# The two adaLN parts of a hybrid diffusion step: matmul rows on four column groups of TensorE instead of one, modulation on VectorE

## The chip, the core and the metric

One core of one Trainium2 chip runs the whole program. The metric is the device time of one execution in microseconds (us). The engines are PE (TensorE: matmuls; PEld are its weight loads), DVE (VectorE), ACT (ScalarE), POOL (GpSimd) and SP (SyncE, which issues most DMAs). All of them run their own list of instructions in order and meet at semaphores.

## What is computed

One layer of a diffusion backbone on 1024 latent tokens and 128 context tokens, width 1024, all in float32. The conditioning vector is multiplied by a 1024 x 6144 matrix, `w_ada`. Of the six slices of the result two (shift `sh1`, scale `sc1`) modulate the input of the first projection, `w_in`; the others are used behind the output projection and the feed-forward part.

```python
def trunk_layer(x, cond, rows, cols, st0, p):
    ada = jax.nn.silu(cond) @ p['w_ada'] + p['b_ada']
    sh1, sc1, g1, sh2, sc2, g2 = jnp.split(ada, 6, axis=-1)
    h = modulate(layer_norm(x), sh1, sc1)        # x * (1 + scale) + shift
    proj = h @ p['w_in']
    ...  # pooling mixer, convolution + bidirectional mLSTM scans, w_out
    x = layer_norm(ALPHA * x + g1[:, None, :] * mix, p['ln1_g'], p['ln1_b'])
    h = modulate(layer_norm(x), sh2, sc2)
    ffn = conv_ffn(h, rows, cols, p['w_up'], p['w_dw'], p['b_dw'], p['w_down'])
    x = layer_norm(ALPHA * x + g2[:, None, :] * ffn, p['ln2_g'], p['ln2_b'])
```

There are two conditioning vectors: `c` for the latent tokens and `c_ctx` for the context tokens. So `silu(cond) @ w_ada` is a product of two rows with a large matrix.

## The kernel before

Order and buffers are written out by hand for each engine; what is said here of an order is the order of that engine's code.

**The start.** SP loads nine token tiles `xt` (128 tokens each), between them the first four of eight loads of `w_ada` (load i: half of the contraction, 512 columns; `ADA1_BLOCKS` says which columns), then two units of `w_in` (`raw`), the last four loads of `w_ada` and two more units. DVE takes the statistics of each tile, ACT normalises it (`x_norm`), PE transposes it (`x_transposes`, eight 128 x 128 matmuls with the identity), and ACT copies the result out of PSUM into `xT` (`xT_evac`).

**adaLN, first part.** Loads 0, 1, 3, 4, 6 and 7 are multiplied on PE (`ada1_rows`): for each of the four 128-row slices in a load one matmul with the two conditioning columns in `colv` as weights and 512 columns of `w_ada` as moving operand. The result, two rows of 512, lies in partitions 0 and 1 of PSUM bank 6. Loads 2 and 5 are instead multiplied and summed on DVE (`ada1_acc`, one accumulator for each conditioning vector), and PE adds the 128 partitions of the accumulators onto the two rows (`ada1_fold`, weights `pick`). ACT copies the two rows into `arow` (`arow_evac`), PE transposes them block by block into bank 7 (`ada1_cols`), and DVE adds the bias (`ada1_evac`), once for each half of the 1024 channels. Then ACT modulates `xT` with scale and shift of each channel (`modulate`) and rounds it (`h1hi`), and DVE makes the rest `h1lo = xT - h1hi`: all large products are made from three fp32r matmuls, hi x hi, hi x lo and lo x hi. `h1_first` does the first of eight channel rows in three token groups, `h1_parts(k)` a whole row.

**First tiles of the projection** (`first_tiles(half, k)`): half 0 makes tiles 0 and 1 with channel rows 0 to 3 as far as row k goes, 18 matmuls of 384 columns; half 1 adds rows 4 to 7 of the other weights. Between them stand `ada1_fold(1)`, the rows of loads 6 and 7 and the last column transposes. Then come the gate columns and the other units of the projection, n = 4 to 31, with three token groups g each.

**adaLN, second part.** DVE multiplies and sums the other 3072 columns of `w_ada` in six blocks j beside the projection (`ada_unit`, 48 of them; each adds one 128-row slice for both conditioning vectors). When a block is summed, PE adds its partitions (`ada2_cols` by way of `acc_cols`, 8 matmuls): the accumulator is the weight, `pick` (two columns) the moving operand, and the result comes out as columns in bank 6. `ADA_COLS` puts the six behind token group 1 of units n = 5, 11, 16, 20 and 28, and behind the first group of the unit after the last. DVE waits for j before it starts the block that reuses the accumulator (`ada_unit`, the wait for `pe_ada`). Another 1024 columns come much later through `acc_cols` too; the change does not touch them.

The functions that the change touches, and what calls them:

Of the kernel before, what the change touches and what calls it, by code (L numbers as in the profile page):

```python
# [10 lines left out]
P = 128  # L11
# [52 lines left out]
ROW_BLOCKS = (2, 0, 3, 1)  # L64
ACC_LOADS = (2, 5)
# [55 lines left out]
def layer(nc, x_prompt, x_sample, c, state_C, state_n, state_m, c_ctx, w_ada, b_ada, w_in, b_gates,  # L121
          w_qk_conv, hn_g, w_pool, pool_scale, w_out, ln1_g, ln1_b, w_up, w_dw, b_dw, w_down,
          ln2_g, ln2_b, inv_count, y_prompt, y_sample, new_C, new_n, new_m, scan_rows, gate_rows, pool_out, x1_rows, u_rows, t_rows):
    with ExitStack() as stack, nc.allow_non_contiguous_dma(reason="normaliser column of the state, stabiliser rows"):
# [77 lines left out]
        grow = place("grow", [1, 2, P])  # L202
        mrow = place("mrow", [1, P])
# [16 lines left out]
        arow = place("arow", [2, 2, AC], tmp_at + 4 * 4 * AC + 8 * AC)  # L220
# [4 lines left out]
        aacc0 = place("aacc0", [P, 2, AC], M0 + 4 * (KT - 1) * T)  # L225
# [238 lines left out]
        nmr_ready, acc1_ready = sem("nmr_ready"), sem("acc1_ready")  # L464
# [4 lines left out]
        (x1_copied, x2_copied), X_0 = d_exp, NT  # L469
        s_kept, kw_kept, KEPT_0 = (ln_ready, exps_ready), (rows_silu, wghi_ready), 1  # L470
# [683 lines left out]
        def _(pe):  # L1154
# [15 lines left out]
            def ada1_rows(i, start):  # L1170

                pe.wait_ge(ada1_in[i % ADA1_RING], 16 * (i // ADA1_RING + 1))
                if start and i:
                    pe.wait_ge(arow_ready, i // 2)
                for k in range(KH):
                    kk = (i % 2) * KH + k
                    last = mm(ps[0:2, 6, :], colv[:, V_C + kk:V_CC + kk + 1:V_CC - V_C], adaw1[:, i % ADA1_RING, k, :],
                              start=(start and k == 0), stop=(not start and k == KH - 1))
                last.then_inc(pe_ada, 1)

            def ada1_fold(a):

                pe.wait_ge(acc1_ready, a + 1)
                for w in both:
                    last = mm(ps[0:2, 6, :], pick[:, w, :], (aacc0, aacc)[a][:, w, :], start=False, stop=(w == 1))
                last.then_inc(pe_ada, 1)

            def ada1_cols(j):

                pe.wait_ge(arow_ready, j + 1)  # L1190
                if j == 2:
                    pe.wait_ge(ada_a, 1)
                for b in range(AB):
                    blk = ROW_BLOCKS[j] * AB + b
                    last = nc.tensor.transpose(ps[:, 7, 2 * blk:2 * blk + 2], arow[:, j % 2, b * P:(b + 1) * P],
                                               ident[0:2, 0:2])
                return last
# [23 lines left out]
            ada1_fold(0)  # L1221
            x_transposes(8)
            ada1_cols(1).then_inc(pe_adaT, 1)
            ada1_rows(4, True)

            def ada2_cols(j):

                pe.wait_ge(ada_used, 4 * (j + 1))
                acc_cols(6, 2 * (4 + j) * AB, [ada_sum(j)[:, w, :] for w in both]).then_inc(pe_ada, 1)
# [557 lines left out]
        def _(act):  # L1787
# [36 lines left out]
            def modulate(k, spans):  # L1824
                for w, tok_ in spans:
                    last = fn(xT[:, k, tok_], xT[:, k, tok_], ACT.Identity,
                              scale=ada1p[:, 0, k, w:w + 1], bias=adaT[:, A_SH1 + k, w:w + 1])
                last.then_inc(mod_ready, 1)

            def h1_first():  # L1830
                act.wait_ge(xT_out, NT)
                act.wait_ge(ada_a, 1)
                for g in range(NG):
                    modulate(0, [(0, grp(g))] if g < NG - 1 else [(0, slice(g * GN, LAT)), (1, slice(LAT, T))])
                    act.wait_ge(mod_ready, g + 1)
                    fn(h1hi[:, 0, grp(g)], xT[:, 0, grp(g)], ACT.Copy).then_inc(h1hi_ready, 1)

            def h1_parts(k):
                if k == KH:
                    act.wait_ge(ada_a, 2)  # L1840
                modulate(k, ((0, slice(0, LAT)), (1, slice(LAT, T))))
# [27 lines left out]
            arow_evac(3)  # L1869
            for k in range(KH, KT):  # L1870
                h1_parts(k)
# [51 lines left out]

            for n in range(4, 2 * NPROJ):
# [42 lines left out]
            silu(2 * H - 1)  # L1967

# [710 lines left out]
        def _(dve):  # L2679
# [8 lines left out]
            v.memset(neghalf[:, :, :], -0.5).then_inc(ones_ready, 1)  # L2688

# [29 lines left out]
            def ada1_evac(half):  # L2719
                dve.wait_ge(pe_adaT, half + 1)  # L2720
                ada_evac(7, A_SH1 + half * KH, A_SH1 + (half + 1) * KH)
# [831 lines left out]
```

## Time and profile before

| | |
|---|---|
| time, median of 3 runs | 1291.76 us (1289.9 to 1292.05) |
| the profiled execution's own time | 1290.97 us |
| its span, first to last instruction | 1289.2 us |
| PE busy | 1241.7 us (96% of the span), 7531 matmul records |
| DVE busy | 1011.9 us (78%) |
| ACT busy | 583.2 us (45%) |
| POOL busy | 652.7 us (51%) |
| DMA | 210.25 MB, 163 GB/s in the mean |

The rest of 1.8 us lies around the span. A float32 matmul is two records on PE, each with a weight load; an fp32r matmul and a transpose are one. Times in rows count from the start of the span. A record of PE contains its way through the array, so records overlap: what one costs in a stream is the distance from its start to the next one's.

### The profile page before, as it was taken

How to read it: one execution, taken by the hardware profiler on the slowest of the kernel's cores; microseconds unless marked ns; L12 is line 12 of the kernel's file. 1: busy time of each engine (PE TensorE's matmuls, PEld its weight loads, DVE VectorE, ACT ScalarE, POOL GpSimd, SP SyncE). 2: the span in 40 equal slices, each digit the busy share in tenths (PEclk: the TensorE clock that was granted, in tenths of full speed). 3: DMA queues.
4: the chain of work that ended last, by engine and by line, in shares of the span. 5: the costliest groups of instructions: out<-in, count | busy, mean ns of one | idle time of the engine just before them, and what ended most of it. 6: DMA issues, size and time to landing. Idle time of an engine off the chain costs nothing.

```text
span 1289.2 us, 21414 instructions
## 1 busy us (share of the span) xinstructions
PE 1241.7 (96%) x7531; PEld 1131.1 (88%) x7531; DVE 1011.9 (78%) x1556; ACT 583.2 (45%) x1013; POOL 652.7 (51%) x519
## 2 busy tenths in 40 slices
PE   6899999999988999998999999999999999999996
PEld 3488899999987778998999999999999988888885
DVE  6466688965688788799878787878866599889898
ACT  5644112536546444555454444445434456345430
POOL 1001999604343011369798888879787764200011
PEclk9999999999999999999999999999999999999999
DMA  9524232463336532213635353544534669946882
GB/s 359 167 77 144 61 111 87 144 191 83 94 105 233 175 115 78 70 33 120 190 122 187 130 180 122 179 161 142 165 135 150 219 231 382 329 131 208 300 315 100
DMA packets 161777, 210.25 MB, mean 163 GB/s; under 512 B 10567, under 2 KB 98723, under 8 KB 161443
## 3 DMA queue, kind: packets, MB, share of 16 engines
q1 hardware_dynamic: 161214, 204.47, 48.3%
q0 software_dynamic: 288, 4.72, 0.9%
q8 instruction: 44, 0.72, 0.2%
q14 instruction: 34, 0.28, 0.1%
q10 hardware_dynamic: 197, 0.06, 0.0%
HBM read 161.49 MB, written 47.72 MB: 162 GB/s over the span
## 4 chain that ended last, share of the span: by engine, by line
PE 52%; POOL 2%; DVE 1%; issue 1%; ACT 0%; POOLq 0%
PE ps L1693 11%; PE ps L1691 11%; PE ps L1692 11%; PE ps L1724 6%; PE ps L1726 6%; PE ps L1725 6%; POOL tlo L2387 0%; POOL ulo L2387 0%; POOL xlo L2387 0%; POOL dwlo L2387 0%; POOL xwlo L2387 0%; PE ps L1203 0%; POOL wsum L2592 0%; DVE z L3434 0%; DVE z L3433 0%
## 5 line engine op out<-in xcount | busy, mean ns | idle before, releaser
L3248 DVE SCALAR_TENSOR_TENSOR ps<-gs,taps,ps 128x945 f32<-128x945 f32 (+2 forms) x176 | 215.7, 1226 | 10.0 <-ACT ps L2165 4.6
L2534 POOL TENSOR_TENSOR rstd<-mv,neghalf 128x1 f32<-128x1 f32 x27 | 24.8, 918 | 258.2 <-DVE mv L3425 156.9
L1296 PE MATMUL ps<-h1hi,whi 128*128 128x384 f32 x336 | 118.5, 353 | 0.9 <-DVE wlo L2731 0.9
L1724 PE MATMUL ps<-dwhi,uhi 128*128 128x512 f32 x290 | 113.0, 390 | 1.3 <-POOL dwlo L2387 1.3
L1726 PE MATMUL ps<-dwhi,ulo 128*128 128x512 f32 x290 | 112.9, 389 | 0.0
L1725 PE MATMUL ps<-dwlo,uhi 128*128 128x512 f32 x290 | 112.9, 389 | 0.0
L1296 PE MATMUL ps<-h1hi,wlo 128*128 128x384 f32 x336 | 112.5, 335 | 0.0
L1296 PE MATMUL ps<-h1lo,whi 128*128 128x384 f32 x336 | 112.4, 335 | 0.0
L2387 POOL TENSOR_TENSOR wlo<-raw,whi 128x512 fp32r<-128x512 f32 x40 | 57.2, 1431 | 80.8 <-ACT whi L1796 48.0
L1691 PE MATMUL ps<-thi,xhi 128*128 128x288 f32 x320 | 94.3, 295 | 2.0 <-issue 1.1
L1693 PE MATMUL ps<-thi,wlo 128*128 128x288 f32 x320 | 94.4, 295 | 0.0
L1693 PE MATMUL ps<-thi,xlo 128*128 128x288 f32 x320 | 94.4, 295 | 0.0
L1692 PE MATMUL ps<-tlo,whi 128*128 128x288 f32 x320 | 94.2, 294 | 0.0
L1692 PE MATMUL ps<-tlo,xhi 128*128 128x288 f32 x320 | 94.2, 294 | 0.0
L1691 PE MATMUL ps<-thi,whi 128*128 128x288 f32 x320 | 94.1, 294 | 0.0
L1691 PE MATMUL ps<-h2hi,whi 128*128 128x288 f32 x240 | 71.5, 298 | 1.0 <-POOL wlo L2387 1.0
L1691 PE MATMUL ps<-h2hi,xhi 128*128 128x288 f32 x240 | 70.8, 295 | 1.2 <-POOL xlo L2387 1.2
L1693 PE MATMUL ps<-h2hi,wlo 128*128 128x288 f32 x240 | 71.4, 298 | 0.0
L1692 PE MATMUL ps<-h2lo,whi 128*128 128x288 f32 x240 | 71.4, 298 | 0.0
L1693 PE MATMUL ps<-h2hi,xlo 128*128 128x288 f32 x240 | 70.8, 295 | 0.0
L1692 PE MATMUL ps<-h2lo,xhi 128*128 128x288 f32 x240 | 70.7, 294 | 0.0
L3292 DVE TENSOR_TENSOR val<-val,ps 128x576 f32<-128x576 f32 x20 | 15.1, 754 | 65.2 <-PE ps L1693 65.2
(464 smaller groups left out, 4031.8 us busy)
## 6 DMA issues: line engine op xcount, KB each, us to landing
raw<-in_w_up SPq DMA_DIRECT2D x78, 256.0 KB, 4.8
u_rows<-val SPq DMA_DIRECT2D x22, 576.0 KB, 2.9
adaw<-in_w_ada SPq DMA_DIRECT2D x24, 512.0 KB, 4.0
st<-in_w_down SPq DMA_DIRECT2D x22, 512.0 KB, 4.3
t_rows<-st SPq DMA_DIRECT2D x11, 1024.0 KB, 4.6
raw<-in_w_in SPq DMA_DIRECT2D x40, 256.0 KB, 4.2
w_raw<-in_w_down SPq DMA_DIRECT2D x33, 256.0 KB, 6.0
v_raw<-u_rows SPq DMA_DIRECT2D x33, 256.0 KB, 5.8
```

The costliest lines, as they stand in the source:

```text
L1296: last = mm(ps[:, bank, 0:GN], a[:, n % 2, k * P:(k + 1) * P], b[:, kk, grp(g)], start=(kk == 0 and a is whi and b is h1hi), stop=(kk == K ...
L1691: mm(out, hi_w[:, ks], b_hi[:, k, cols], start=(n < 2 and k == 0), stop=False, skip_group_check=True)
L1692: mm(out, hi_w[:, ks], b_lo[:, k, cols], start=False, stop=False, skip_group_check=True)
L1693: last = mm(out, lo_w[:, ks], b_hi[:, k, cols], start=False, stop=(k == KH - 1), skip_group_check=True)
L1724: mm(out, u_hi, w_hi, start=start, stop=False, skip_group_check=True)
L1725: mm(out, u_hi, w_lo, start=False, stop=False, skip_group_check=True)
L1726: return mm(out, u_lo, w_hi, start=False, stop=stop, skip_group_check=True)
L2387: return nc.gpsimd.tensor_tensor(out, full, hi_part.bitcast(F32), ALU.subtract)
L2534: tt(rstd[:, j % 4, :], mv[:, j % 4, 1:2], neghalf[:, 0, :], ALU.pow).then_inc(rstd_ready, 1)
L3248: step(stt(a3[:, ro, co], g3[:, ri, ci], taps[:, tap:tap + 1], a3[:, ro, co], ALU.mult, ALU.add), 2 + m)
L3292: tt(c22, c22, ps[:, PB:PB + 2, 0:TC], ALU.add).then_inc(c22_added, 1)
```

## The change

1. `ada1_rows` multiplies all eight loads. Each matmul of 512 columns becomes four of 128 columns. The four outputs, two partitions each, begin at partitions 0, 32, 64 and 96, so each is made by another column group of the array, 32 columns wide. `ada1_acc`, `ada1_fold` and their accumulator are gone, from DVE and PE.
2. `arow_evac` copies 128 partitions x 128 columns instead of 2 x 512; `ada1_cols` is one 128 x 128 transpose of it instead of four with two partitions; `ada1_evac` picks two of each 32 rows out of the result. The places of the rows in PE's list change: 0, 1, 2 and 3 between the transposes of the tokens, 4 and 5 behind `first_tiles(0, 0)`, 6 and 7 where they were. The order of the loads stays.
3. `modulate` moves from ACT to DVE (`tensor_scalar`, multiply and add).
4. In the second part the accumulators become the moving operand: `ada2_rows(j)` is 8 matmuls with the two columns of `pick` as weights and 128 columns of the accumulator, again on four column groups, behind token group 0. ACT copies the rows out (`frow_evac`), and `ada2_cols(j)` is one matmul with these as weights and eight columns of the identity as moving operand, behind token group 2. Block 5 has them behind the last group of one unit and the first of the next.
5. DVE clears bank 6 once at the start.

```diff
-            def ada1_rows(i, start):
+            def ada1_rows(i):
 
                 pe.wait_ge(ada1_in[i % ADA1_RING], 16 * (i // ADA1_RING + 1))
-                if start and i:
-                    pe.wait_ge(arow_ready, i // 2)
+                j, half = i // 2, i % 2
+                if j and not half:
+                    pe.wait_ge(arow_ready, j)
                 for k in range(KH):
-                    kk = (i % 2) * KH + k
-                    last = mm(ps[0:2, 6, :], colv[:, V_C + kk:V_CC + kk + 1:V_CC - V_C], adaw1[:, i % ADA1_RING, k, :],
-                              start=(start and k == 0), stop=(not start and k == KH - 1))
+                    kk = half * KH + k
+                    for q in range(QUADS):
+                        last = mm(ps[32 * q:32 * q + 2, 6, j * P:(j + 1) * P], colv[:, V_C + kk:V_CC + kk + 1:V_CC - V_C],
+                                  adaw1[:, i % ADA1_RING, k, q * P:(q + 1) * P], start=(kk == 0), stop=(kk == KT - 1))
                 last.then_inc(pe_ada, 1)
...
+            def ada2_rows(j):
+
+                pe.wait_ge(ada_used, 4 * (j + 1))
                 for w in both:
+                    for q in range(QUADS):
+                        last = mm(ps[32 * q:32 * q + 2, 6, 3 * P:4 * P], pick[:, w, :], ada_sum(j)[:, w, q * P:(q + 1) * P],
+                                  start=(w == 0), stop=(w == 1))
                 last.then_inc(pe_ada, 1)
...
+            def ada2_cols(j):
+
+                pe.wait_ge(frow_ready, FR_0 + j + 1)
+                last = mm(ps[:, 6, 2 * (4 + j) * AB:2 * (5 + j) * AB], frow[:, :], row_pick, start=True, stop=True)
...
             pe.wait_ge(xT_out, NT)
             first_tiles(0, 0)
-            ada1_fold(1)
+            ada1_rows(4)
+            ada1_rows(5)
             first_tiles(0, 1)
-            ada1_rows(6, True)
-            ada1_rows(7, False)
+            ada1_rows(6)
+            ada1_rows(7)
...
-                if g == 1 and n in ADA_COLS:
+                if g == 0 and n in ADA_COLS:
                     if n > POOL_FIRST:
                         pe.wait_ge(po_ready, min(2 * (n - POOL_FIRST), 12))
+                    ada2_rows(ADA_COLS[n])
+                if g == 2 and n in ADA_COLS:
                     ada2_cols(ADA_COLS[n])
...
-            h1_first()
-            h1_parts(1)
+            for g in range(NG):
+                h1_hi_first(g)
             arow_evac(2)
-            for k in range(2, KH):
-                h1_parts(k)
+            for k in range(1, KH):
+                h1_hi(k)
+            arow_evac(3)
...
+                if n in ADA_COLS:
+                    frow_evac(ADA_COLS[n])
...
+            def modulate(k, spans):
+                for w, tok_ in spans:
+                    last = tsc(xT[:, k, tok_], xT[:, k, tok_], ada1p[:, 0, k, w:w + 1], adaT[:, A_SH1 + k, w:w + 1],
+                               ALU.mult, ALU.add)
+                last.then_inc(mod_ready, 1)
...
-            for i in range(KH):
-                ada1_acc(0, i)
-            ada1_acc(1, 0)
-            ada1_acc(1, 1)
             lo(0)
             lo(1)
             ada1_evac(0)
+            dve.wait_ge(xT_out, NT)
+            modulate_first(0)
+            modulate_first(1)
             h1_lo_first(0)
-            ada1_acc(1, 2)
+            modulate_first(2)
             h1_lo_first(1)
-            ada1_acc(1, 3)
+            modulate_row(1)
             h1_lo_first(2)
-            for k in range(1, KH):
-                h1_lo(k)
+            for k in range(2, KH):
+                modulate_row(k)
+                h1_lo(k - 1)
+            h1_lo(KH - 1)
```

Three places show how the lists move. PE at the start of the program, before (`ident,xt` are the token transposes, `adaw_79,colv` the rows of a load, `aacc_116,pick` the first fold, `ident,arow` the column transposes):

```order
L1164 MATMUL ps<-ident,xt 128x128 x16
L1177 MATMUL ps<-adaw_79,colv 2x512 x4
L1195 MATMUL ps<-ident,arow 128x2 x4
L1164 MATMUL ps<-ident,xt 128x128 x16
L1185 MATMUL ps<-aacc_116,pick 2x512 x2
L1164 MATMUL ps<-ident,xt 128x128 x8
L1195 MATMUL ps<-ident,arow 128x2 x4
L1177 MATMUL ps<-adaw_79,colv 2x512 x4
L1245 MATMUL ps<-h1hi,whi 128x384
```

and now:

```order
L1165 MATMUL ps<-ident,xt 128x128 x16
L1180 MATMUL ps<-adaw_79,colv 2x128 x16
L1187 MATMUL ps<-ident,arow 128x128
L1165 MATMUL ps<-ident,xt 128x128 x16
L1180 MATMUL ps<-adaw_79,colv 2x128 x16
L1165 MATMUL ps<-ident,xt 128x128 x8
L1187 MATMUL ps<-ident,arow 128x128
L1248 MATMUL ps<-h1hi,whi 128x384
```

The rows of load 4, which stood between the last column transpose and the first tile of the projection, no longer stand there.

ACT before, behind the three token groups of channel row 0 (`arow` is a row copy, `h1hi` of 1152 columns a whole channel row, `wearly` the rounding of two units of weights):

```order
L1836 ACTIVATE h1hi<-xT 128x384
L1826 ACTIVATE xT<-xT,adaT,ada1p 128x1024
L1826 ACTIVATE xT<-xT,adaT,ada1p 128x128
L1843 ACTIVATE h1hi<-xT 128x1152
L1818 ACTIVATE arow<-ps 2x512
L1826 ACTIVATE xT<-xT,adaT,ada1p 128x1024
L1826 ACTIVATE xT<-xT,adaT,ada1p 128x128
L1843 ACTIVATE h1hi<-xT 128x1152
```

and now:

```order
L1833 ACTIVATE h1hi<-xT 128x384 x3
L1825 ACTIVATE arow<-ps 128x128
L1837 ACTIVATE h1hi<-xT 128x1152 x3
L1825 ACTIVATE arow<-ps 128x128
L1842 ACTIVATE wearly<-raw 128x512 x2
L1837 ACTIVATE h1hi<-xT 128x1152 x4
```

The row copy that waits for loads 4 and 5 now stands ahead of channel row 1, not behind it; and the modulations are gone from this list.

ACT before, at units 5 and 6 of the projection (`Wr` are the exponential and the logarithm of the gates, `qk` the copy of a finished tile):

```order
L1933 ACT_TABLE_LOAD
L1933 ACTIVATE Wr<-lf 128x128
L1934 ACT_TABLE_LOAD
L1934 ACTIVATE Wr<-Wr 128x128
L1796 ACTIVATE whi<-raw 128x512
L1956 ACTIVATE qk<-ps 128x1152
```

and now:

```order
L1931 ACT_TABLE_LOAD
L1931 ACTIVATE Wr<-lf 128x128
L1932 ACT_TABLE_LOAD
L1932 ACTIVATE Wr<-Wr 128x128
L1920 ACTIVATE frow<-ps 128x128
L1803 ACTIVATE whi<-raw 128x512
L1956 ACTIVATE qk<-ps 128x1152
```

The copy of the rows of block 0 stands behind the gates' exponential and logarithm.

## Rows read from the trace of the kernel before

**Rows 1.** The page, busy time, share of the span and instructions of engines.

```profile
PE 1241.7 (96%) x7531; PEld 1131.1 (88%) x7531; DVE 1011.9 (78%) x1556; ACT 583.2 (45%) x1013; POOL 652.7 (51%) x519
```

**Rows 2.** Timeline of PE: start us, us, engine, line, operation, count, [idle before, releaser].

```profile
26.40 3.60 PE L1177 MATMUL ps<-adaw,colv 128*2 128x512 f32 x8
...
36.01 0.41 PE L1195 MATMUL ps<-ident,arow 2*128 2x2 f32 x4 [0.95 <-ACT arow L1818]
36.35 3.60 PE L1177 MATMUL ps<-adaw,colv 128*2 128x512 f32 x8
40.51 0.41 PE L1245 MATMUL ps<-h1hi,whi 128*128 128x384 f32 x1 [0.56 <-DVE h1lo L2740]
...
44.13 0.55 PE L1245 MATMUL ps<-h1hi,whi 128*128 128x384 f32 x1 [1.00 <-DVE h1lo L2740]
...
47.98 1.88 PE L1185 MATMUL ps<-aacc,pick 128*2 128x512 f32 x4
...
53.13 7.03 PE L1177 MATMUL ps<-adaw,colv 128*2 128x512 f32 x16
...
61.86 0.65 PE L1195 MATMUL ps<-ident,arow 2*128 2x2 f32 x8
...
67.37 0.44 PE L1245 MATMUL ps<-h1hi,wearly 128*128 128x384 f32 x1
```

**Rows 3.** Timeline of ACT, normalising, row copies, modulation and rounding.

```profile
22.75 1.24 ACT L1822 ACTIVATE xt<-xt,nmr,rstd 128x1024 f32<-128x1024 f32 x1
...
26.56 1.23 ACT L1822 ACTIVATE xt<-xt,nmr,rstd 128x1024 f32<-128x1024 f32 x1
27.69 1.01 ACT L1813 ACTIVATE xT<-ps 128x1024 f32<-128x1024 f32 x1
28.59 1.23 ACT L1822 ACTIVATE xt<-xt,nmr,rstd 128x1024 f32<-128x1024 f32 x1
...
38.44 0.71 ACT L1826 ACTIVATE xT<-xT,adaT,ada1p 128x384 f32<-128x384 f32 x1 [1.58 <-DVE ada1p L2724]
...
43.84 1.17 ACT L1843 ACTIVATE h1hi<-xT 128x1152 fp32r<-128x1152 f32 x1
49.89 0.59 ACT L1818 ACTIVATE arow<-ps 2x512 f32<-2x512 f32 x1 [4.89 <-PE ps L1185]
```

**Rows 4.** Busy time by stretch: PE, PEld, DVE, ACT, POOL, granted clock, DMA.

```profile
44.00:47.60 3.60, 3.47 (x11) 3.47 (x12) 1.44 (x2) 1.00 (x1) 0.00 (x0) 0.54 0.99 317
```

**Rows 5.** Groups by shape on PE: busy us, mean ns of one, idle before.

```profile
L1288 PE MATMUL ps<-ident,graw 32*128 32x32 f32 x9 | 0.7, 224 | 0.7 <-DVE graw L2785 0.7
...
L1309 PE MATMUL ps<-ident,gcol 128*1 128x128 f32 x4 | 0.6, 271 | 0.0
```

**Rows 6.** Timeline of DVE, an accumulation and a row of `h1lo`.

```profile
34.32 0.88 DVE L2755 TENSOR_SCALAR aacc<-adaw,colv 128x512 f32<-128x512 f32 x2 [2.37 <-DMA adaw<-in_w_ada]
...
53.23 1.36 DVE L2744 TENSOR_TENSOR h1lo<-xT,h1hi 128x1152 fp32r<-128x1152 f32 x1 [6.83 <-ACT h1hi L1843]
```

**Rows 7.** Timeline of PE at units 5 and 7 of the projection.

```profile
100.42 0.33 PE L1296 MATMUL ps<-h1hi,wlo 128*128 128x384 f32 x1
100.59 1.84 PE L1203 MATMUL ps<-pick,aacc 128*128 128x2 f32 x16
102.30 0.42 PE L1296 MATMUL ps<-h1hi,whi 128*128 128x384 f32 x1
102.56 0.33 PE L1296 MATMUL ps<-h1lo,whi 128*128 128x384 f32 x1
...
111.73 0.45 PE L1296 MATMUL ps<-h1hi,whi 128*128 128x384 f32 x1 [0.86 <-DVE wlo L2731]
```

**Rows 8.** Timeline of DVE at unit 5, the first accumulation of block 1.

```profile
102.55 0.88 DVE L2907 TENSOR_SCALAR aacc<-adaw,colv 128x512 f32<-128x512 f32 x2 [4.67 <-PE ps L1203]
```

**Rows 9.** Timeline of ACT at unit 5, the gates' exponential and logarithm.

```profile
105.76 0.31 ACT L1933 ACTIVATE Wr<-lf 128x128 f32<-128x128 f32 x1 [7.38 <-DVE lf L2809]
...
107.39 0.31 ACT L1934 ACTIVATE Wr<-Wr 128x128 f32<-128x128 f32 x1
```

More of the change, by code:

```diff
@@ L202, in layer @@
         grow = place("grow", [1, 2, P])
+        frow = place("frow", [P, P], SBUF_END - 4 * P)
         mrow = place("mrow", [1, P])
@@ L1190, in ada1_cols @@
                 pe.wait_ge(arow_ready, j + 1)
[L1191 to L1197, printed above, removed]
+                return nc.tensor.transpose(ps[:, 7, j * P:(j + 1) * P], arow[:, j, :], ident[:, :])
+            row_pick = ident[:, :].rearrange("p (q n) -> p q n", q=QUADS)[:, :, 0:2]
+            def ada2_rows(j):
+                pe.wait_ge(ada_used, 4 * (j + 1))
+                for w in both:
+                    for q in range(QUADS):
+                        last = mm(ps[32 * q:32 * q + 2, 6, 3 * P:4 * P], pick[:, w, :], ada_sum(j)[:, w, q * P:(q + 1) * P],
+                                  start=(w == 0), stop=(w == 1))
+                last.then_inc(pe_ada, 1)
+            def ada2_cols(j):
+                pe.wait_ge(frow_ready, FR_0 + j + 1)
+                last = mm(ps[:, 6, 2 * (4 + j) * AB:2 * (5 + j) * AB], frow[:, :], row_pick, start=True, stop=True)
+                if j == N_ADA2 - 1:
+                    last.then_inc(pe_adaT, 1)
             def acc_cols(bank, col, acc):
@@ L1220, in _ @@
             x_transposes(7)
-            ada1_fold(0)
+            ada1_rows(3)
             x_transposes(8)
             ada1_cols(1).then_inc(pe_adaT, 1)
[L1224 to L1229, printed above, removed]
             def first_tiles(half, k, tiles=(0, 1)):
@@ L1822, in x_norm, with h1_hi_first, h1_hi @@
                 fn(xt[:, t, :], xt[:, t, :], ACT.Identity, scale=rstd[:, t % 4, :], bias=nmr[:, t % 4, :]).then_inc(xn_ready, 1)
[L1824 to L1841, printed above, removed]
+            def h1_hi_first(g):
+                act.wait_ge(mod_ready, g + 1)
+                fn(h1hi[:, 0, grp(g)], xT[:, 0, grp(g)], ACT.Copy).then_inc(h1hi_ready, 1)
+            def h1_hi(k):
                 act.wait_ge(mod_ready, NG + k)
@@ L1922, in v_evac, with frow_evac @@
                 fn(v1[:, t, :, 0:P], ps[:, t % (2 * NG), :].rearrange("p (h n) -> p h n", h=H), ACT.Copy).then_inc(v_ready, 1)
+            def frow_evac(j):
+                act.wait_ge(pe_ada, N_ADA1 + j + 1)
+                fn(frow[:, :], ps[:, 6, 3 * P:4 * P], ACT.Copy).then_inc(frow_ready, 1)
             for n in range(4, 2 * NPROJ):
@@ L2720, in ada1_evac @@
                 dve.wait_ge(pe_adaT, half + 1)
[L2721 to L2722 removed]
+                for j in (2 * half, 2 * half + 1):
+                    b0 = ADA1_BLOCKS[j] * AB
+                    last = tt(adaT[:, b0:b0 + AB, :], ps[:, 7, j * P:(j + 1) * P].rearrange("p (b q) -> p b q", b=QUADS)[:, :, 0:2],
+                              bc(colv[:, V_BADA + b0:V_BADA + b0 + AB].unsqueeze(2), [P, AB, 2]), ALU.add)
+                link(last)
                 ks = slice(half * KH, (half + 1) * KH)
@@ L2914, in ada_unit @@
                     link(last)
-            h1_lo(5)
-            ada_unit(0)
-            h1_lo(6)
-            ada_unit(1)
-            h1_lo(7)
-            ada_unit(2)
-            ada_unit(3)
+            h1_lo(KT - 1)
+            for u in range(4):
+                ada_unit(u)
             lo(4)
```

60 lines of the change are left out of this document (25 added, 35 removed).

## The prediction

> **What bounds the kernel now.** The page comes first: PE is busy for 96% of the span [rows 1]. So work taken off PE counts, and so does idle time of PE; a gain on another engine counts only where PE waits for it. The change touches the first 67 us and six places in the projection, so I read the timelines there. Up to 36 us PE is full of token transposes and adaLN rows: a load's eight records take 3.60 us, 0.43 from start to start [rows 2]. From 36.01 to 40.51 it waits for the way column transposes, bias on DVE, modulation on ACT (from 38.44), rounding, `h1lo`; the rows of load 4 (36.35) fill most of that wait [rows 2, 3]. Then come three token groups with gaps of about 1 us before two of them, and then a stretch at half clock: 0.54 granted on average between 44.0 and 47.6, that is 1.2 GHz for nearly all of it, after PE had been little busy; 3.6 x (1 - 0.54) = 1.7 us lost against 2.4 GHz [rows 2, 4]. From 47.98 to 67.37, the start of half 1, PE never waits: a fold (1.8 us), the rows of loads 6 and 7 (7.0), column transposes (0.6) and 54 tile matmuls 0.17 apart.
>
> **The unknown price: a record on a column group.** A load now takes 16 matmuls, 32 records of 128 columns with two columns of weights. The nearest row for one record is L1309 (one weight column, 128 moving columns, always the same column group): four records in 0.6 us with 0.271 of flight, so (0.6 - 0.27)/3 = 0.11 us [rows 5], a quarter of the 0.43 above. If the groups don't overlap, a load costs R = 32 x 0.108 = 3.5 us as before. The lower end: the two records of one float32 matmul share a group and follow each other, so only the second of one and the first of the next can overlap if PE starts its records in order: 16 x 0.107 = 1.7 us. The shortest distance between records with a weight load of their own in these rows is L1288's (0.7 - 0.22)/8 = 0.06 [rows 5], so 32 x 0.062 = 2.0 us. I take R = 2.0, the row nearest in kind (small records, each with its load), with 1.7 and 3.5 as bounds.
>
> If all four groups ran at once whatever the order, R would be 32/4 x 0.108 = 0.9. The Trainium skill, "TensorE: Matmul & The Clock Gate", section "Part 3: Packing small matmuls", has that: matmuls in different column groups start some 4 ns apart. No row of before shows two groups in use, so it is a rival below.
>
> **The start, step by step.** (a) Up to the first tile. With R = 2.0 PE no longer sets the pace, ACT does. From 22.75 it still has four normalisations (1.13 each, 26.56 to 27.69), five `xT` copies (0.90, 27.69 to 28.59), two roundings of 512 columns of weights (0.5 each, after the 1.17 for 1152) and two row copies (0.25 each, now 128 columns): 10.5 us, to 33.4 [rows 3]. The columns are ready by then (rows of load 3 end near 31, the last transposes near 33), so DVE modulates from 33.5, against ACT's 38.44. From there DVE takes 0.4 for a group of 384 columns (the 0.44 for 512 of L2755 [rows 6] less a quarter, plus overhead), then rounding 0.45, `h1lo` 0.5 and the steps between engines: 1.85 us against the 2.07 from 38.44 to 40.51. First tile at 35.4: **5.1 us earlier**. (b) The gaps before groups 1 and 2: modulation and rounding now lie on two engines, so group 2 is there 2.4 us after group 0, not 3.6: **1.2 earlier**. PE is as little busy around this place as before, so I keep one half-clock stretch and its 1.7 us. (c) Behind tile row 0 the rows of loads 4 and 5 take 2R = 4.0 where the fold took 1.8: **2.2 later**. Their data landed by 34.3 (DVE's wait for load 5 ended then [rows 6]). (d) A new wait. ACT's copy of these rows now stands ahead of the rounding of channel row 1, and the copy waits for both loads; behind it wait `h1hi`, DVE's `h1lo` and PE's tile row 1. From the end of PE's rows: 0.25 copy, 1.1 `h1hi`, 1.3 `h1lo` [rows 3, 6], 0.4 for four hand-overs: **3.1 later**, and nothing else stands in PE's list to fill it. Before, ACT had the same copy at 49.89 but row 1 was done. (e) Rows of loads 6 and 7: 2R = 4.0 against 7.0: **3.0 earlier**. (f) Column transposes about even; DVE's second half (bias 0.5, modulation 0.95, two weight splits 1.3, the next modulation 0.95, `h1lo` 1.3, ACT's rounding beside them) ends 0.4 us after PE wants row 4: **0.4 later**. Further rows take DVE 0.95 + 1.28 = 2.2 us each against PE's 3.1, so they don't wait. (g) PE idles 3.1 us in (d); a second half-clock stretch (1.3 to 1.7 us) is about even odds: **0.6 later**. Sum: 5.1 + 1.2 - 2.2 - 3.1 + 3.0 - 0.4 - 0.6 = **3.0 us earlier** at the start of half 1. Behind it PE is the bound and the other engines follow its list, so this stays.
>
> The accumulations taken off DVE (16 instructions) and the modulations taken off ACT free time that nobody waits for beyond what (a) counts. The clearing of bank 6 lies in DVE's wait for the first tile: nothing.
>
> **The second part.** Before, one block costs 1.71 us (100.59 to 102.30), 16 records at 0.107, plus 0.09 on the first matmul behind it (0.26 to the next start, 0.17 in a stream) [rows 7]: 1.8. Now: 16 records at 0.062 = 1.0, the two of `ada2_cols` with a full weight load 0.2, and three more or less sharp changes of shape at 0.09: 1.5. Gain 0.3 x 6 = **1.9 us**.
>
> The Trainium skill, "TensorEngine Tiling (Array Packing)", section "Key Properties", speaks against this: a change of tiling mode drains TensorE. The row shows 0.09 for a change of shape; if a change cost the 0.25 us that a record spends in flight, 18 changes would cost 2.9 us more and the six blocks would lose 1 us.
>
> Unit 5 is special. ACT's `frow` copy stands behind the gates' logarithm. DVE waits for block 0 at PE (4.67 us, until 102.55), then takes 3.2 us to the gates' input, ACT 0.3 + 1.28 (its table) + 0.3 to the end of the logarithm at 107.7 [rows 8, 9]. `pe_ada` now comes behind group 0, near 99.6 in that clock, so DVE goes 2.8 us earlier and `frow` is copied by 105.2; PE has finished groups 1 and 2 (2.1 each) at 103.8. It waits **1.5 us**, and the old wait of 0.86 at unit 7, the end of the same chain, disappears [rows 7]: net 0.6 lost. At the other five places ACT is free well inside the two groups (at unit 28 its copy comes some 2 us before PE needs it). Second part: 1.9 - 0.6 = **1.3 us** gained.
>
> **Sum.** 3.0 + 1.3 = 4.3 us from the profiled execution's own 1290.97: 1286.7. That execution lies 0.8 below the median of 1291.76; halfway between the two bases I say 1287.0.
>
> **Rivals.** *Serial groups*: the records don't overlap, R = 3.46. Then PE paces the start again, the first tile is 1.7 earlier instead of 5.1, (c) costs 5.1, (d) stays, (e) gives nothing: 1.7 + 1.2 - 5.1 - 3.1 = 5.3 later. A block then costs 1.73 + 0.2 + 0.27 = 2.2: 2.4 lost, with unit 5 3.0. Together 8.3: 1299.3. It decides from R = 2.6, 81 ns a record, on: from R = 2.0 each us of R costs 4 in (c) and (e) and 3 in the blocks, so the 4.3 are gone there. For it: every record here with this shape takes 108 ns. Against it: those were all on one group. *All four at once*: R = 0.9. (a) and (b) stay, ACT is the bound; (c) is even, (e) gives 5.2, so 8 us at the start; blocks 6 x 0.9 less 0.6: 4.7. Together about 12: 1279. For it speaks the rule above, against it that the two records of a matmul share a group. *Nothing measurable*: records at 70 to 80 ns, or dear mode changes (2.9), or both half-clock stretches in full: 1289.5 to 1293.
>
> **How the numbers follow.** Forecast 0.54, serial 0.25, nothing measurable 0.15, all at once 0.06. A change under 0.2% (2.6 us) can't be told from none here. Forecast and all-at-once count as faster: 0.60; same 0.15; slower 0.25. The forecast's own range is 1284 (R = 1.7, one stretch) to 1289. The range that leaves out the all-at-once case and the dearer part of the serial one is 1282.5 to 1299.5.
>
> **What would show it.** Right: L1180's 32 records of a load in about 2 us; first tile near 35.4; an idle stretch of about 3 us on PE ahead of tile row 1, released by `h1lo`; half 1 starting near 64; 1.5 us of PE waiting for `frow` at unit 5 and none at unit 7. Wrong: records 108 ns apart (then slower), a load under 1.2 us, the gain lost later in a stage where PE waits for POOL or a load.

## The result: 1278.6 us, and the profile after

The changed kernel takes 1278.62 us (median of 4 runs, 1278.45 to 1280.09), the kernel before 1291.9 in the same comparison: a ratio of 0.9901, with a 95% interval from 0.9889 to 0.9914. It is faster, as forecast, but by 13 us instead of 4.3: outside the range of 1282.5 to 1299.5 and at the 1279 of the rival "all four at once", which had been given 0.06.

The profiled execution took 1278.46 us, 12.51 less than the one of before. Two places in TensorE's (PE's) timeline split that. The start of half 1 moved from 67.37 [rows 2] to 59.51, 7.86 earlier; the other 4.65 come between there and the columns of the last block (282.1 us). Behind that, up to the stores, the two traces run side by side to within 0.2 us.

The page, busy time and share of each engine, against [rows 1]:

```profile
PE 1222.6 (96%) x7731; PEld 1127.2 (88%) x7731; DVE 1008.7 (79%) x1559; ACT 570.2 (45%) x1001; POOL 652.7 (51%) x519
```

PE has 200 matmul records more and is busy 19 us less: the first sign that records lie on top of each other. PE is still the bound at 96%.

PE's timeline up to the start of half 1 and at unit 5, the places of [rows 2] and [rows 7] (start us, duration us, engine, line, operation, count, [idle before, releaser]). L1180 are the rows of the loads, L1187 the column transposes, L1248 the first tiles, L1300 the projection's tiles, L1196 and L1203 the second part's rows and columns:

```profile
24.89 1.63 PE L1180 MATMUL ps<-adaw,colv 128*2 128x128 f32 x32
...
29.50 1.06 PE L1180 MATMUL ps<-adaw,colv 128*2 128x128 f32 x32
...
35.85 0.66 PE L1248 MATMUL ps<-h1hi,whi 128*128 128x384 f32 x1 [2.52 <-DVE h1lo L2757]
...
42.37 1.93 PE L1180 MATMUL ps<-adaw,colv 128*2 128x128 f32 x64
47.14 0.45 PE L1248 MATMUL ps<-h1hi,whi 128*128 128x384 f32 x1 [2.84 <-DVE h1lo L2761]
...
50.49 1.93 PE L1180 MATMUL ps<-adaw,colv 128*2 128x128 f32 x64
...
54.03 0.38 PE L1187 MATMUL ps<-ident,arow 128*128 128x128 f32 x2
...
59.51 0.45 PE L1248 MATMUL ps<-h1hi,wearly 128*128 128x384 f32 x1 [0.21 <-DVE h1lo L2761]
...
90.48 0.34 PE L1300 MATMUL ps<-h1hi,wlo 128*128 128x384 f32 x1
90.75 0.62 PE L1196 MATMUL ps<-aacc,pick 128*2 128x128 f32 x16
...
96.88 0.39 PE L1203 MATMUL ps<-ident,frow 128*128 128x8 f32 x2 [1.15 <-ACT frow L1920]
```

Two loads' rows, 64 records, take 1.93 us from the first start to the last end; before, the 16 wide records of loads 6 and 7 took 7.03. Less the flight of the last record (0.27, of which 0.11 is its turn), a load costs (1.93 - 0.16)/2 = 0.89 us, not the 2.0 of the prediction. The new wait ahead of tile row 1 (47.14) and the one for `frow` at unit 5 (96.88) are both there.

Why a load is so cheap is seen by counting the records in flight. The rows of loads 4 and 5 in short windows 0.109 us apart, then in one (stretch, length, PE busy with the count of records, granted clock, DMA):

```profile
42.37:42.40 0.03, 0.03 (x4) 1.00 0.00 0
42.48:42.51 0.03, 0.03 (x8) 1.00 0.00 0
42.59:42.61 0.03, 0.03 (x12) 1.00 0.00 0
42.37:44.24 1.87, 1.87 (x64) 1.00 0.86 185
```

The count is of the records that lie in the window, so it holds those still in flight; each of the first three windows adds four. In the trace their starts are 42.371, 42.377, 42.384 and 42.391, then 42.480 to 42.500: four records 6 to 7 ns apart, the next four 0.109 us later. So a load is eight rounds of four, 8 x 0.109 = 0.87 us. The Trainium skill, "TensorE: Matmul & The Clock Gate", section "Part 3: Packing small matmuls", gives some 4 ns between starts in different column groups; the trace agrees in kind, with 6 to 7.

What holds the wait at 47.14, on ACT and DVE:

```profile
44.37 0.28 ACT L1825 ACTIVATE arow<-ps 128x128 f32<-128x128 f32 x1 [7.53 <-PE ps L1180]
44.54 2.21 ACT L1837 ACTIVATE h1hi<-xT 128x1152 fp32r<-128x1152 f32 x2
```

```profile
45.73 1.36 DVE L2761 TENSOR_TENSOR h1lo<-xT,h1hi 128x1152 fp32r<-128x1152 f32 x1 [6.55 <-ACT h1hi L1837]
```

ACT has stood idle for 7.53 us in front of the copy of rows that PE finished at 44.3; only behind it comes the rounding of channel row 1, whose data had been modulated since 37.7, and behind that DVE's remainder.

### The profile page after: what moved, and what is told of

The parts are those of the page before. It is cut to its first block, busy times and chain, and to the rows that moved or that the text cites. A ratio compares the mean times of both kernels' runs of the same rounds, so it can differ in the third digit from the quotient of the medians.

```text
span 1276.7 us, 21799 instructions
## 1 busy us (share of the span) xinstructions
PE 1222.6 (96%) x7731; PEld 1127.2 (88%) x7731; DVE 1008.7 (79%) x1559; ACT 570.2 (45%) x1001; POOL 652.7 (51%) x519
## 4 chain that ended last, share of the span: by engine, by line
PE 52%; POOL 2%; DVE 1%; issue 1%; ACT 0%; POOLq 0%
PE ps L1700 11%; PE ps L1698 11%; PE ps L1699 11%; PE ps L1733 6%; PE ps L1732 6%; PE ps L1731 6%; POOL tlo L2388 0%; POOL ulo L2388 0%; POOL xlo L2388 0%; POOL dwlo L2388 0%; POOL xwlo L2388 0%; PE ps L1211 0%; POOL wsum L2593 0%; DVE z L3435 0%; DVE z L3434 0%
## 5 line engine op out<-in xcount | busy, mean ns | idle before, releaser
L1300 PE MATMUL ps<-h1hi,whi 128*128 128x384 f32 x336 | 118.7, 353 | 0.0
L1300 PE MATMUL ps<-h1hi,wlo 128*128 128x384 f32 x336 | 112.5, 335 | 0.0
L1300 PE MATMUL ps<-h1lo,whi 128*128 128x384 f32 x336 | 112.4, 335 | 0.0
```

The costliest lines, as they stand in the source:

```text
L1300: last = mm(ps[:, bank, 0:GN], a[:, n % 2, k * P:(k + 1) * P], b[:, kk, grp(g)], start=(kk == 0 and a is whi and b is h1hi), stop=(kk == K ...
```

## Experiments: is it the groups?

The theory is that all of the gain at the start follows from R, the time of a load's rows, and that R is small because the four column groups run side by side. The rival is that the reordering (no fold, modulation on DVE, copies moved) brings it.

**All sixteen matmuls of a load on one group.**

```diff
-  last = mm(ps[32 * q:32 * q + 2, 6, j * P:(j + 1) * P], colv[:, V_C + kk:V_CC + kk + 1:V_CC - V_C],
-            adaw1[:, i % ADA1_RING, k, q * P:(q + 1) * P], start=(kk == 0), stop=(kk == KT - 1))
+  last = mm(ps[0:2, 6, j * P:(j + 1) * P], colv[:, V_C + kk:V_CC + kk + 1:V_CC - V_C],
+            adaw1[:, i % ADA1_RING, k, q * P:(q + 1) * P], start=(kk == 0 and q == 0), stop=(kk == KT - 1 and q == QUADS - 1))
```

> The first part's sixteen matmuls of a load all write column group 0 (all four quarters into the same two rows, so the adaLN row holds their sum and not the four quarters); everything else as in the changed kernel. Theory A (the gain at the start is the four column groups running at once): the records follow each other at 0.108 us, a load takes 32 x 0.108 = 3.5 us instead of 1.0, PE paces the start again, and half 1 starts about 13 us later than the changed kernel's 59.5, near 72.5, so the time is near 1291.5. Rival B (the gain at the start is the reordering: no fold, modulation on DVE, copies moved): half 1 starts within 3 us of 59.5 and the time is below 1282.

Measured: 1295.44 us (1292.78 to 1297.71), ratio to the kernel before 1.0031 [1.0021, 1.0040]. Its PE timeline, and the count of records in windows 0.109 apart:

```profile
40.62 0.41 PE L1248 MATMUL ps<-h1hi,whi 128*128 128x384 f32 x1 [2.83 <-DVE h1lo L2757]
...
46.65 7.15 PE L1180 MATMUL ps<-adaw,colv 128*2 128x128 f32 x64
56.61 0.69 PE L1248 MATMUL ps<-h1hi,whi 128*128 128x384 f32 x1 [2.81 <-DVE h1lo L2761]
```

```profile
46.65:46.67 0.03, 0.03 (x1) 1.00 1.27 473
46.76:46.78 0.03, 0.03 (x2) 1.00 0.76 276
46.87:46.89 0.03, 0.03 (x3) 1.00 1.20 453
```

One record is added each 0.109 us and a load takes (7.15 - 0.16)/2 = 3.50. Half 1 starts at 75.54, later than in the kernel before. So the rival falls: without the groups the rest of the first part's change costs time, and even the second part's gain doesn't make up for it. The expectation was 4 us short in the time, and 3 at the start of half 1 (72.5 expected), which comes 16.0 later than in the changed kernel: the first tile, at 40.62, is 4.8 of these, the two pairs of loads are 5.2 each, and behind the wait at 56.61 the tiles run at half clock for a while (0.69 instead of 0.45 for the first).

**Two groups.** The same edit with `32 * (q % 2)` as the first row.

> The first part's matmuls of a load alternate between column groups 0 and 1 only (quarters 0 and 2 are summed into the first, 1 and 3 into the second, so the adaLN row is not the reference's); everything else as in the changed kernel. Theory A (each group takes one record in 0.109 us, and groups run side by side in this order): 16 x 0.109 = 1.75 us a load; by the step from the changed kernel (0.95 us a load) to the group-by-group order (2.07 us, 5.5 us later), 4.9 us for each us of a load, so 1282.5. Rival B (only a matmul's second record overlaps the next one's first): 24 records' time or more, 2.6 us a load, 1287.

Measured: 1282.17 us (1280.65 to 1284.44), ratio 0.9928 [0.9906, 0.9949].

```profile
41.12 3.66 PE L1180 MATMUL ps<-adaw,colv 128*2 128x128 f32 x64
```

(3.66 - 0.16)/2 = 1.75 us a load, half of the one-group time: each group takes one record in 0.109 us, and two run side by side. Theory A's numbers hold, 1.75 and 1282.5.

**Four groups, but written group by group.** The same sixteen matmuls and the same results; only the two loops are exchanged.

```diff
-  for k in range(KH):
-      kk = half * KH + k
-      for q in range(QUADS):
+  for q in range(QUADS):
+      for k in range(KH):
+          kk = half * KH + k
```

> The first part computes the same, but a load's matmuls are written group by group (four rounds for group 0, then four for group 1, ...) and not round by round. Theory A1 (each column group has its own queue, whatever the order in the program): a load stays at 1.0 us and the time at 1278.6. Theory A2 (TensorE starts records in program order, so only neighbours of different groups overlap): three of 32 records overlap, a load takes 29 x 0.108 = 3.1 us, half 1 starts near 71 and the time is near 1290. Between the two: a short look-ahead, a load of 1.5 to 2.5 us, 1281 to 1287.

Measured: 1284.16 us (1281.78 to 1286.87), ratio 0.9941 [0.9920, 0.9962]. The rows of loads 4 and 5 on PE, and the records in flight in the rows of loads 6 and 7:

```profile
42.15 4.18 PE L1180 MATMUL ps<-adaw,colv 128*2 128x128 f32 x64
49.13 0.69 PE L1248 MATMUL ps<-h1hi,whi 128*128 128x384 f32 x1 [2.81 <-DVE h1lo L2761]
```

```profile
54.02:54.05 0.03, 0.03 (x1) 1.00 0.00 0
54.35:54.38 0.03, 0.03 (x3) 1.00 0.00 0
54.46:54.49 0.03, 0.03 (x4) 1.00 0.00 0
54.57:54.60 0.03, 0.03 (x5) 1.00 0.00 0
57.88:57.91 0.03, 0.03 (x3) 1.00 0.00 0
```

The first four records start alone, 0.109 apart; from 54.461 on two start in each turn (54.461 and 54.466), 28 times, and the last four are alone again: 36 turns of 0.109, so 2.0 us a load. Neither of the pure theories holds. Groups are not independent whatever the order (then 0.87), and records are not simply started in the order of the program (then 3.1). A record doesn't name its matmul in the trace; the counts fit if the next group's first record starts while the group ahead has four of its eight left (4 turns, and 4 for each of the eight groups of two loads: 36). How far PE looks ahead and by what rule stays open; that the order within the program is worth 1.1 us a load is shown.

**Each part alone.** The changed kernel with the second part of before, and the kernel before with the changed second part (with bank 6 cleared once, as in the change):

```diff
-  if g == 0 and n in ADA_COLS:
...
-      ada2_rows(ADA_COLS[n])
-  if g == 2 and n in ADA_COLS:
+  if g == 1 and n in ADA_COLS:
...
       ada2_cols(ADA_COLS[n])
...
-  last = mm(ps[:, 6, 2 * (4 + j) * AB:2 * (5 + j) * AB], frow[:, :], row_pick, start=True, stop=True)
+  acc_cols(6, 2 * (4 + j) * AB, [ada_sum(j)[:, w, :] for w in both]).then_inc(pe_ada, 1)
```

> The changed kernel with the accumulator columns of the kernel before in the second part (sixteen matmuls with two moving columns a block, no row copy). Theory A (all groups at once in both parts; traces put 7.9 us of the gain before the start of half 1 and 4.7 behind it): 1278.6 + 4.7 = 1283.3. Rival C (the second part is worth only the 1.3 us of the prediction and the rest behind 59.5 us comes from the start): 1280.0.

> The kernel before with the changed second part alone (rows on four groups, the row copy, two transposing matmuls a block; bank 6 cleared once). Theory A (the two parts add up): 4.7 us less than the kernel before, 1287.2. Rival B (behind the slower start the gates' chain is late at unit 5 or 7 in another way): 1288.5 or more.

Measured: 1283.71 us (1282.73 to 1284.14), ratio 0.9935 [0.9918, 0.9951], and 1286.48 us (1285.53 to 1291.40), ratio 0.9963 [0.9948, 0.9978]. The two gains, 8.2 and 5.3 against the kernel before in the same comparisons (1291.9 and 1291.81), add to 13.5; the whole change has 13.3. So no effect of one part on the other is seen; the intervals of the two ratios leave room for some 2 us of it.

**The second part on one group.**

```diff
-  last = mm(ps[32 * q:32 * q + 2, 6, 3 * P:4 * P], pick[:, w, :], ada_sum(j)[:, w, q * P:(q + 1) * P],
-            start=(w == 0), stop=(w == 1))
+  last = mm(ps[0:2, 6, 3 * P:4 * P], pick[:, w, :], ada_sum(j)[:, w, q * P:(q + 1) * P],
+            start=(w == 0 and q == 0), stop=(w == 1 and q == QUADS - 1))
```

> The second part's eight matmuls of a block all write column group 0 (the four quarters are summed into the same two rows); everything else as in the changed kernel. Theory A: 16 records at 0.108 instead of four rounds of 0.109, 1.73 instead of 0.45 us a block, so 6 x 1.3 = 7.8 us later: 1286.4; the wait for the row copy at unit 5 stays near 1.1. Rival D (the blocks' gain is the two transposing matmuls taking the place of sixteen narrow ones and lies elsewhere): within 2 us of 1278.6.

Measured: 1287.19 us (1286.33 to 1291.67), ratio 0.9960 [0.9946, 0.9974]; 8.6 more than the changed kernel.

```profile
93.25 1.91 PE L1196 MATMUL ps<-aacc,pick 128*2 128x128 f32 x16
```

1.91 instead of 0.62 us for a block's rows; 6 x 1.29 = 7.7. (The profiled execution took 1291.67 us; its half 1 starts at 62.00, 2.5 later than in the changed kernel, so the stage behind that is compared.) From the columns of block 0 to those of block 5 this kernel takes 191.8 us, the changed one 185.2: 1.3 for each of the five blocks between. So here, too, it is the groups.

**Modulation back on ACT.** In `h1_hi_first` and `h1_hi` ACT modulates ahead of each rounding, as in the kernel before; DVE's `modulate_first` and `modulate_row` go.

> The changed kernel with the modulation of the channel rows on ACT ahead of each rounding, as in the kernel before, instead of on DVE. Theory A (the modulation's move shortens the way to the first tiles): a gap near 1 us is back ahead of token groups 1 and 2, and behind the copy of rows 4 and 5 another 1.1 us of modulation stands before tile row 1, so half 1 starts 3 us later and the time is 1281.6. Rival B (the groups give all of the gain, the modulation's place nothing): 1278.6.

Measured: 1281.56 us (1279.98 to 1283.04), ratio 0.9914 [0.9893, 0.9936].

```profile
36.36 0.69 PE L1248 MATMUL ps<-h1hi,whi 128*128 128x384 f32 x1 [0.21 <-DVE h1lo L2769]
...
47.37 0.69 PE L1248 MATMUL ps<-h1hi,whi 128*128 128x384 f32 x1 [4.49 <-DVE h1lo L2773]
```

The total is as expected, half 1 starts 2.6 later, but the terms are others. The gap ahead of token group 1 is 0.21 us, not 1. The wait ahead of tile row 1 grew from 2.84 to 4.49, since the modulation now stands in ACT's list behind the copy. And the clock lies elsewhere (the stretches of tile rows 0 and 1: length, busy time of PE, PEld, DVE, ACT, POOL, granted clock, DMA):

```profile
35.40:41.00 5.60, 5.29 (x22) 4.21 (x26) 1.11 (x2) 1.71 (x4) 0.00 (x0) 0.70 1.01 289
47.40:53.40 6.00, 6.00 (x18) 5.59 (x18) 2.72 (x2) 3.89 (x5) 0.00 (x0) 0.50 0.46 164
```

Tile row 0 runs partly at 2.4 GHz here, tile row 1 at 1.2, where the changed kernel has row 0 at 1.2 and row 1 at 2.4: its row 0 takes 6.52 us up to the rows against 5.56 here, its row 1 3.35 up to the next rows against 6.06. So 1.65 us of wait is what the modulation's place is shown to be worth; the rest of the 2.9 between the medians isn't split by a run of its own; in the two traces it lies where the clock differs. The larger part of the first part's 8 us is the groups'.

## Experiments: the two new waits

**The copy of rows 4 and 5 behind channel row 1.** On ACT:

```diff
-  arow_evac(2)
-  for k in range(1, KH):
+  h1_hi(1)
+  arow_evac(2)
+  for k in range(2, KH):
       h1_hi(k)
```

> The changed kernel with ACT's copy of the rows of loads 4 and 5 put behind the rounding of channel row 1 instead of ahead of it. Theory A: the 2.84 us for which TensorE waits ahead of tile row 1 is ACT's order alone, since nothing in channel row 1 needs these rows; the wait goes, half 1 starts near 56.7 instead of 59.5, and the time is 1275.8. Rival B: DVE (modulation 1.06 and remainder 1.36 us a row) is late next, row 1 is there less than 1 us earlier, 1277.6 or more. Rival C: the clock gives the gain back in a longer half-clock stretch: 1278.

Measured: 1275.14 us (1275.00 to 1275.97), ratio 0.9868 [0.9853, 0.9883].

```profile
42.15 1.93 PE L1180 MATMUL ps<-adaw,colv 128*2 128x128 f32 x64
44.01 0.44 PE L1248 MATMUL ps<-h1hi,whi 128*128 128x384 f32 x1
```

Tile row 1 follows the rows at once, half 1 starts at 56.37, 3.1 earlier than in the changed kernel, and the time is 3.5 less. The wait was ACT's order alone; nothing is late in its place. (The changed kernel was timed in the first comparison only. The kernel before took 1291.9 there and 1293.5 in the one of this section, so a difference of medians from the changed kernel can be off by some 2 us here; the traces are the firmer measure.)

**The rows of loads 4 and 5 ahead of the first tile.**

```diff
   pe.wait_ge(xT_out, NT)
-  first_tiles(0, 0)
   ada1_rows(4)
   ada1_rows(5)
+  first_tiles(0, 0)
   first_tiles(0, 1)
```

> The changed kernel with the rows of loads 4 and 5 ahead of the first tile row instead of behind it, where TensorE is idle for 2.52 us. Theory A: load 5 lands near 34.3, its rows end at 35.4, the first tile stays at 35.85, the 1.93 us behind tile row 0 and the 2.84 us wait behind them both go, as the copy finds its rows done: 4.8 earlier, 1273.8. Rival B: the first tile moves by the rows (to 36.5 or later) and DVE is late next for row 1: 1276.5. In the trace the rows ahead of the first tile either shorten the half-clock stretch from 35.5 to 42.3 us (then up to 2 us more) or not.

Measured: 1270.72 us (1269.67 to 1273.76), ratio 0.9840 [0.9822, 0.9858]; 7.9 less than the changed kernel. Its PE timeline, and two stretches of it (stretch, length, busy time of PE, PEld, DVE, ACT, POOL, granted clock, DMA):

```profile
33.20 3.58 PE L1180 MATMUL ps<-adaw,colv 128*2 128x128 f32 x64 [0.58 <-ACT xT L1820]
36.71 0.44 PE L1248 MATMUL ps<-h1hi,whi 128*128 128x384 f32 x1
...
43.16 1.93 PE L1180 MATMUL ps<-adaw,colv 128*2 128x128 f32 x64
...
52.17 0.44 PE L1248 MATMUL ps<-h1hi,wearly 128*128 128x384 f32 x1 [0.21 <-DVE h1lo L2761]
```

```profile
33.20:36.70 3.50, 3.50 (x64) 2.17 (x64) 3.26 (x9) 1.46 (x3) 0.00 (x0) 0.51 1.05 386
36.70:43.10 6.40, 6.40 (x40) 6.20 (x36) 6.40 (x10) 3.71 (x4) 0.00 (x0) 1.00 0.91 216
```

The rows fill the idle time ahead of the first tile, which comes 0.86 later (rival B was right in that), and both the 1.93 us behind tile row 0 and the wait go. The other 3.4 us are the clock (tile rows 0 and 1 take 6.45 us together instead of 6.52 and 3.35): the half-clock stretch, 1.2 GHz, falls on the rows (0.51 granted), and the tiles run at 2.4 GHz from the first on; in the changed kernel the whole of tile row 0 ran at 1.2 GHz. Half 1 starts 7.3 earlier than there.

**The copy of block 0's rows ahead of the gates.** On ACT, at unit 5, `frow_evac` goes ahead of the exponential and the logarithm.

```diff
   if n == 5:
+      frow_evac(ADA_COLS[n])
       act.wait_ge(f_abs, 1)
```

> The changed kernel with ACT's copy of block 0's rows at unit 5 put ahead of the gates' exponential and logarithm. Theory A: TensorE's wait of 1.15 us for that copy goes and nothing takes its place: 1277.5. Rival B: the end of the gates' chain is late again at unit 7 (0.86 us in the kernel before): 1278.3.

Measured: 1278.04 us (1276.83 to 1279.68), ratio 0.9889 [0.9872, 0.9906]: by the time alone no difference from the changed kernel's 1278.62. The trace shows more. On ACT and on PE:

```profile
92.56 0.28 ACT L1920 ACTIVATE frow<-ps 128x128 f32<-128x128 f32 x1 [2.21 <-PE ps L1196]
```

```profile
96.70 0.28 PE L1203 MATMUL ps<-ident,frow 128*128 128x8 f32 x2
```

The 1.15 us wait is gone, no wait came in at unit 7, and from the start of half 1 to the last block's columns PE takes 221.2 us instead of 222.6. But this execution has a half-clock stretch from 48.0 to 51.4 that the profiled one of the changed kernel hasn't, and half 1 starts 1.1 later. The stretch:

```profile
48.00:51.40 3.40, 3.40 (x13) 3.14 (x11) 2.29 (x2) 0.90 (x1) 0.00 (x0) 0.54 0.64 224
```

The gain is shown in its stage and not in the total.

**All three edits together.**

> All three edits together: rows of loads 4 and 5 ahead of the first tile row, their copy behind channel row 1's rounding, block 0's row copy ahead of the gates' exponential. Theory A: the gains that don't overlap add up, 4.8 + 1.1: 1272.7. Rival B (DVE or the clock takes part of it back): 1275 to 1277.

Measured: 1270.74 us (1270.38 to 1271.65), ratio 0.9835 [0.9822, 0.9849]. This is as fast as the rows moved alone, not 1.1 faster. Half 1 starts at 52.24 (52.17 there), the last block's columns come at 273.5 (274.8 there), so 1.3 us are in hand at that point; then this execution loses them between 940 and 960 us, where it has a half-clock stretch and the other none. The windows, of the rows moved alone and of all three together:

```profile
940.00:960.00 20.00, 20.00 (x156) 20.00 (x157) 14.20 (x17) 8.04 (x14) 14.01 (x11) 1.00 0.55 188
```

```profile
940.00:960.00 20.00, 20.00 (x143) 20.00 (x143) 12.92 (x16) 6.49 (x11) 13.48 (x11) 0.91 0.56 188
```

20 x (1 - 0.91) = 1.8 us. The stretch is not of this version's making: ten of the thirteen profiled executions have one between 941 and 971 us, those of the kernel before and of the changed kernel among them; the rows moved alone, the copy behind channel row 1 and the two-group kernel have none. The changed kernel, and three windows of the kernel before:

```profile
940.00:960.00 20.00, 20.00 (x146) 20.00 (x146) 8.84 (x14) 7.45 (x12) 15.97 (x13) 0.91 0.43 137
```

```profile
930.00:960.00 30.00, 30.00 (x231) 30.00 (x229) 22.25 (x26) 13.98 (x24) 23.21 (x19) 1.00 0.40 137
960.00:962.00 2.00, 2.00 (x20) 2.00 (x20) 0.87 (x1) 1.09 (x2) 2.00 (x2) 1.00 0.00 0
962.00:966.00 4.00, 4.00 (x21) 4.00 (x21) 1.84 (x4) 0.00 (x0) 3.77 (x4) 0.57 0.36 147
```

So the execution of the rows moved alone was lucky there, by some 1.5 us; of the 8.8 by which it is shorter than that of the changed kernel, the edit's share is the 7.3 at the start of half 1. The 1.3 of the other edits are shown in their stage; that the medians are level is explained by this for the two profiled executions only. Both versions take 1.6% less than the kernel before, and 8 us less than the changed one; of these two I'd keep the simpler, the rows moved alone.

## Why the prediction was wrong, by its steps

The step that failed is the price of a record, R. The forecast took 2.0 us a load, with a lower bound of 1.7 from the argument that the two records of one float32 matmul share a group and that PE starts records in order, so that at most two overlap. Measured is 0.89. The records in flight show four starting within 20 ns; the argument against the rival was an inference from rows in which only one group was ever used, and it should have been a rival with an even chance and not a bound. The forecast sat at R = 2.0 by the distance of L1288's records [rows 5]; their shape, `32*128 32x32`, is 128 weight columns, the whole width of the array, and 32 moving columns, a quarter of what a record streams here, so it says nothing on several groups. The experiment with the loops exchanged (2.0 us a load) has just that R in the first part, with the second part at its measured price. With the second part's 1.3 replaced by the 4.65 measured behind the start of half 1, the forecast of 1287.0 becomes 1283.7; that kernel took 1284.2. So the sum was about right for the R that it was given.

(a) First tile at 35.4, with ACT as the pace: measured 35.85, 4.66 earlier than before against 5.1. Right; PE is idle for 2.52 us there. The rest is a half-clock stretch from 25.3 to 28.7 (0.51 granted, below): in the kernel with the second part on one group, whose program is the same up to there and which hasn't got it, the first tile starts at 35.14.

(b) Tile row 0 was to lose 1.2 us of gaps and keep one half-clock stretch. Measured: 6.52 us from first tile to rows (35.85 to 42.37) against 7.47 before, so 0.95 earlier, but made up otherwise. These windows of the changed kernel show the clock around it:

```profile
25.30:28.70 3.40, 3.40 (x35) 2.83 (x28) 0.76 (x5) 2.79 (x4) 0.55 (x1) 0.51 1.11 341
35.60:42.30 6.70, 6.33 (x18) 5.34 (x18) 3.58 (x9) 0.52 (x1) 0.00 (x0) 0.50 0.85 237
47.10:50.10 3.00, 2.96 (x17) 2.96 (x18) 3.00 (x4) 1.18 (x1) 0.00 (x0) 1.00 1.03 367
```

Half clock lasts for 6.7 us behind 2.52 us of idle time, 6.7 x 0.5 = 3.35 lost instead of the 1.7 of [rows 4]; the gaps closed by more than thought: no idle time of 0.2 us or more is left ahead of token groups 1 and 2.

(c) Rows of loads 4 and 5 for the fold: 1.93 against 1.88, even, not 2.2 later: the R term. (d) The new wait: 2.84 us against 3.1, by the chain that was named (copy, rounding, remainder). Right, and shown by the copy's move. (e) Rows of loads 6 and 7: 5.1 us earlier (7.03 to 1.93), not 3.0: the R term again. (f) PE waits 0.21 us for DVE's remainder of row 4 ahead of half 1, against 0.4. (g) No half-clock stretch behind the 2.84 us wait in this execution (1.00 granted in the third row above), against 0.6 at even odds; two-group, group-by-group and `frow`-ahead executions have one at that very place. Sum: 4.66 + 0.95 - 0.05 - 2.84 + 5.1 = 7.8, measured 7.86, forecast 3.0. Of the 4.9 between, 4.25 are (c) and (e).

Second part: a block's rows with the change of shape on both sides delay the tile matmuls behind them by 0.75 us, its columns by 0.23, where the sixteen old matmuls delayed them by 1.79: 0.8 a block, 4.8 for six, against 0.3 and 1.9. R again: four rounds of four records take 0.44, not 1.0. Changes of shape cost 0.1 each (0.27 instead of 0.17 from the last tile matmul at 90.48 to the first row), as in [rows 7]. The Trainium skill, "TensorEngine Tiling (Array Packing)", section "Key Properties", has a drain at a change of mode; the trace bounds it at these 0.1 us. Unit 5: a wait of 1.15 us for `frow`, 1.5 forecast, and the 0.86 at unit 7 gone; both right, by the chain that was told.

The rival "all four at once" had every term at R = 0.9 and came to 1279; measured 1278.6. "Serial groups" is shown false for this kernel. Its price of 1299.3 was too low: the first part on one group costs 16.8 us more than the changed kernel, the second 8.6, together 1304.0 if the two add, which is an estimate.

## What to carry to other kernels

Small matmuls with few weight columns belong on different column groups, and the order in the program counts: go round the groups with consecutive matmuls. Here that is 0.89 us for sixteen float32 matmuls, against 2.0 group by group and 3.50 on one group.

Work that has become cheap should then be moved into PE's idle time, and what waits for it put behind what doesn't: two such edits, each alone and without one instruction less, gave another 7.9 and 3.5 us. A bound that rests on how an engine is thought to start its work, with no row that shows it in use, is no bound; it needs a rival with a fair chance, or a range that reaches past it.

## What the runs showed of the hardware that I had not expected

- The two records of a float32 matmul don't hold up the other groups: four records start within 20 ns, and again each 0.109 us. With the matmuls in group order two start per 0.109 us.
- The same instructions with the same idle time before them ran at either clock. Behind the wait of 2.8 us ahead of tile row 1 the changed kernel was granted 1.00; the kernel with the second part on one group, whose program is the same up to there, had 0.50 from 47.0 to 52.5, 2.75 us lost. From 25.3 to 28.7 it is the other way round, 0.51 in the changed kernel and 1.00 in that one. Its windows:

```profile
25.30:28.70 3.40, 2.45 (x41) 1.92 (x31) 0.78 (x5) 3.40 (x4) 0.55 (x1) 1.00 1.12 344
47.00:52.50 5.50, 5.50 (x17) 5.50 (x18) 3.45 (x4) 1.16 (x1) 0.00 (x0) 0.50 0.57 198
```

What decides it the runs don't show. The stretches measured here cost 1.7 to 3.4 us, so an edit worth 1 us is seen in its stage and not in the total. The spread between executions goes with the clock: of the ten with the second part alone, those of 1291.3 and 1291.4 us were granted 0.993 and 0.991 in the mean, the others, up to 1287.5, 0.995 to 0.997.
- Idle time ahead isn't needed for a half-clock stretch. In the kernel before PE was busy through all of 930 to 966 us (the windows above) and was granted 0.57 from 962 to 966, that is 1.2 GHz for most of it.
- A half-clock stretch cost least where it fell on rows of few weight columns that fill idle time: with the rows of loads 4 and 5 ahead of the first tile it fell on them, and the tiles ran at full clock.
